# Attention and state space steps moved between the quarters of the projection

## What is computed

```python
h = x @ w_in
z, xbc, dt_raw, q, k, v = _split(h, [1024, 1536, 16, 512, 512, 512])
xbc = jax.nn.silu(_causal_depthwise_conv(xbc, conv_w, conv_b))        # 4 taps
dt = jax.nn.softplus(dt_raw + dt_bias); a = -jnp.exp(a_log)
y = _ssd_scan(xs, dt, a, bs, cs)                                      # 16 heads of 64, 2 groups
y = _rms_norm((y + d_skip * xs) * jax.nn.silu(z), norm_g)
# stick-breaking attention, 8 heads of 64, strictly causal:
#   A[t,s] = sigmoid(z_ts) * prod_{s<j<t} (1 - sigmoid(z_tj))
return jnp.concatenate([y, sb], axis=-1) @ w_out
```

## Time and profile before

| | us |
|---|---|
| median of 3 runs | 2407.09 (2406.55 to 2411.23) |
| the profiled execution, its own time | 2406.45 |
| its span in the trace | 2404.6 |
| PE busy in the span | 2195.6 |
| DVE busy | 1760.2 |
| ACT busy | 1399.7 |
| mean granted clock of TensorE | 0.945 |

### The profile page before, as it was taken

How to read it: one execution, slowest core, us unless ns; L and a number is a source line. 1 busy time by engine, 2 the same in 40 slices (tenths; PEclk the granted TensorE clock), 3 DMA queues, 4 the chain that set the end, 5 groups by cost and what they waited for, 6 DMA issues and landing times.

```text
span 2404.6 us, 31268 instructions
## 1 busy us (share of the span) xinstructions
PE 2195.6 (91%) x9954; PEld 1753.4 (73%) x9954; DVE 1760.2 (73%) x2376; ACT 1399.7 (58%) x1832; POOL 77.2 (3%) x76
## 2 busy tenths in 40 slices
PE   8858899799899797899987799999999999999998
PEld 7846577676677584588776478787878787878886
DVE  5554498764789643445566479898989898989897
ACT  4434277444477340244454168787878787878785
POOL 1000100000100000011110100000000000000000
PEclk9866899999799898999999789999999999999999
DMA  6400588342487242564232089898989898989895
GB/s 237 176 1 0 221 322 335 129 168 108 159 340 280 88 163 92 220 243 174 88 137 74 0 342 376 329 370 326 376 327 377 322 374 323 381 320 380 317 387 220
DMA packets 81542, 577.09 MB, mean 240 GB/s; under 512 B 9408, under 2 KB 9408, under 8 KB 12992
## 3 DMA queue, kind: packets, MB, share of 16 engines
q1 hardware_dynamic: 79888, 570.40, 60.9%
q0 software_dynamic: 1584, 5.77, 0.7%
HBM read 575.08 MB, written 1.05 MB: 240 GB/s over the span
## 4 chain that ended last, share of the span: by engine, by line
PE 77%; DVE 13%; issue 5%; ACT 3%; DMA 1%; POOL 1%; DVEq 0%; SPq 0%; ACTq 0%; POOLq 0%
PE bank L467 21%; PE bank L469 20%; PE bank L468 20%; PE bank L585 6%; PE bank L1221 1%; DVE h L1579 1%; DVE dn_lo L1527 1%; PE bank L1187 1%; DVE pj_lo L504 1%; DVE gu_lo L1527 1%; PE bank L1260 1%; PE bank L572 1%; ACT dn_hi L1364 1%; ACT gu_hi L1356 1%; DMA pieces<-in_pieces 1%
## 5 line engine op out<-in xcount | busy, mean ns | idle before, releaser
L1527 DVE TENSOR_TENSOR gu_lo<-ffw_gu,gu_hi 128x1024 fp32r<-128x1024 f32 x620 | 755.0, 1237 | 145.1 <-ACT gu_hi L1356 130.7
L1356 ACT CAST gu_hi<-ffw_gu 128x1024 fp32r<-128x1024 f32 x620 | 648.1, 1052 | 195.8 <-DMA ffw_gu<-in_gate_up_ff 70.6
L467 PE MATMUL bank<-gu_hi,xg_lo 128*128 128x512 f32 x1152 | 463.0, 402 | 4.5 <-DVE xg_lo L1527 4.3
L469 PE MATMUL bank<-gu_hi,xg_hi 128*128 128x512 f32 x1152 | 452.5, 393 | 0.0
L468 PE MATMUL bank<-gu_lo,xg_hi 128*128 128x512 f32 x1152 | 451.7, 392 | 0.0
L1527 DVE TENSOR_TENSOR dn_lo<-ffw_d,dn_hi 128x1024 fp32r<-128x1024 f32 x299 | 362.7, 1221 | 58.3 <-ACT dn_hi L1364 48.8
L1364 ACT CAST dn_hi<-ffw_d 128x1024 fp32r<-128x1024 f32 x310 | 325.3, 1055 | 95.3 <-PE bank L469 91.6
L467 PE MATMUL bank<-dn_hi,hidt_lo 128*128 128x512 f32 x664 | 265.5, 400 | 28.8 <-DVE hidt_lo L1527 28.8
L469 PE MATMUL bank<-dn_hi,hidt_hi 128*128 128x512 f32 x664 | 259.8, 391 | 0.0
L468 PE MATMUL bank<-dn_lo,hidt_hi 128*128 128x512 f32 x664 | 259.6, 391 | 0.0
L467 PEld LDWEIGHTS bank<-gu_hi,xg_lo 128*128 128x128 f32 x1152 | 217.9, 189 | 48.0 <-DVE xg_lo L1527 5.3
(11 more groups left out here) (394 smaller groups left out, 2852.7 us busy)
## 6 DMA issues: line engine op xcount, KB each, us to landing
ffw_gu<-in_gate_up_m SPq DMA_DIRECT2D x288, 1024.0 KB, 7.0
ffw_d<-in_down_m SPq DMA_DIRECT2D x144, 1024.0 KB, 7.7
pieces<-in_pieces SPq DMA_DIRECT2D x70, 1024.0 KB, 7.1
ffw_gu<-in_gate_up_ff SPq DMA_DIRECT2D x22, 1024.0 KB, 7.0
ffw_d<-in_down_ff SPq DMA_DIRECT2D x11, 1024.0 KB, 8.9
pieces<-in_pieces SPq DMA_DIRECT2D x4, 512.0 KB, 7.3
norm_vec<-in_ln_g POOLq DMA_DIRECT2D x4, 512.0 KB, 4.0
norm_vec<-in_ln_b POOLq DMA_DIRECT2D x4, 512.0 KB, 5.4
```

The source lines that it names most:

```text
L467: nc.tensor.matmul(bank, a_lo, b_hi, start=start, stop=False)
L469: return nc.tensor.matmul(bank, a_hi, b_hi, start=False, stop=stop)
L1356: nc.scalar.copy(gu_hi[:, 2 * k:2 * k + 2, :], ffw_gu[:, blk["slot"], 2 * k:2 * k + 2, :])\
L1527: return V.tensor_tensor(out, x, hi.bitcast(F32), ALU.subtract)
```

## The change

The pieces come in the order q, k, v, dt, xbc (columns 1024 to 1535, which are B and C, first), z, z. A quarter is numbered `at` = 4n + k for piece n and quarter k, 0 to 35. `project_quarter` is the old loop body, and between quarters the engines do:

- the stick-breaking attention in eleven slots (`SB_AT`), from quarter 9 to quarter 21. A head is no longer computed by logarithms. ACT takes two sigmoids of the logits (of z and of -z), DVE forms the product of the (1 - sigmoid)s backward with two `tensor_tensor_scan`s over reversed rows, with a `diagonal` of ones that restarts it, and multiplies; PE turns the weights (three transposes) and ACT copies them out;
- softplus of dt at 16 to 22, with one table that holds exp and ln;
- the convolutions at 20 to 31; their first tap is on ACT (`conv_tap_scalar`), and so are all evacuations of the banks;
- the products of B and C at 25, the first third of `ev_mixT` at 26;
- the state space part for group 0 at 28 to 32 and for group 1 at 33 to 37, five steps (`ssd_tensor`, `ssd_scalar`, `ssd_vector`). The products of `above` and `da` are on ACT (`steps_scalar`, 32 instructions of 128x128) and no more on DVE;
- 36 and 37 lie between the matmuls of the first third of the output, which needs attention alone. The gates, the squares for the rms norm (on ACT) and its roots come there too.

After these, 16 transposes and the other two thirds of the output follow. In the odd mixer a preload of the table with exp and ln is added ahead of its log of the forget gate. Three masks of the attention are gone. The core of the diff:

```diff
@@ -85,14 +85,13 @@
...
-    even = [("z", "tok", columns("ev_w_in", 0, 512), 512), ("z", "tok", columns("ev_w_in", 512, 1024), 512)]
-    even += [("xbc", "feat", columns("ev_w_in", o + 512 * i, o + 512 * (i + 1)), 512) for i in range(3)]
-    o += CONV_DIM
-    even += [("dt", "tok", columns("ev_w_in", o, o + SSD_H), SSD_H)]
-    o += SSD_H
-    even += [("q", "feat", columns("ev_w_in", o, o + 512), 512), ("k", "feat", columns("ev_w_in", o + 512, o + 1024), 512),
-             ("v", "tok", columns("ev_w_in", o + 1024, o + 1536), 512)]
-    even_out = [rows("ev_w_out", k) for k in range(3)]
+    q0 = o + CONV_DIM + SSD_H
+    even = [("q", "feat", columns("ev_w_in", q0, q0 + 512), 512), ("k", "feat", columns("ev_w_in", q0 + 512, q0 + 1024), 512),
+            ("v", "tok", columns("ev_w_in", q0 + 1024, q0 + 1536), 512),
+            ("dt", "tok", columns("ev_w_in", o + CONV_DIM, o + CONV_DIM + SSD_H), SSD_H)]
+    even += [("xbc", "feat", columns("ev_w_in", o + 512 * i, o + 512 * (i + 1)), 512) for i in (2, 0, 1)]
+    even += [("z", "tok", columns("ev_w_in", 0, 512), 512), ("z", "tok", columns("ev_w_in", 512, 1024), 512)]
+    even_out = [rows("ev_w_out", k) for k in (2, 0, 1)]
...
     def project_piece(pe, t, n, first_bank):
 
-            _, kind, g, cols = PLANS[t][n]
-            for k in range(4):
-                if n == 0:
-                    pe.wait_ge(sem("x_split"), DC // 2 * MIXER[t] + k + 1)
...
+        for k in range(4):
+            project_quarter(pe, t, n, k, first_bank)
+
+    def project_quarter(pe, t, n, k, first_bank):
+
+        _, kind, g, cols = PLANS[t][n]
+        if n == 0:
+            pe.wait_ge(sem("x_split"), DC // 2 * MIXER[t] + k + 1)
...
+    EV_N = len(even_pieces)
+    SB_AT = {4 * n + k: i for i, (n, k) in enumerate(((2, 1), (2, 2), (2, 3), (3, 1), (3, 3), (4, 0), (4, 1), (4, 2), (4, 3),
+                                                      (5, 0), (5, 1)))}
+    CONV_AT = 20
+    CONV_ORDER = (8, 9, 10, 11, 0, 1, 2, 3, 4, 5, 6, 7)
+    SSD_AT = (28, 33)
+
+    def ssd_step(at):
+
+        return [(g, at - SSD_AT[g]) for g in range(SSD_G) if 0 <= at - SSD_AT[g] < 5]
+
+    def ssd_tile(g, s):
+
+        return s // 2, 2 * g + s % 2
...
+    def sb_slot_tensor(pe, i):
+        if i < SB_H:
+            if i == 0:
+                pe.wait_ge(sem("const_ready"), 1)
+                read_wait(pe, "ev", 0, 2)
+                read_wait(pe, "ev", 1, 2)
+            if i >= 2:
+                pe.wait_ge(sem("sb_taken"), i - 1)
+            q, kk, bank = (sbq_odd if i % 2 else sbq_even)[:, i // 2, :], sbk[:, i // 2, :], psum[4 + i % 2]
+            nc.tensor.matmul(bank[:, 0:P], q[:, 0:P], kk[:, 0:P], start=True, stop=True)
+            nc.tensor.matmul(bank[:, P:3 * P], q[:, P:S], kk, start=True, stop=True).then_inc(sem("sb_logits"), 1)
+        if 2 <= i < SB_H + 2:
...
+            if v >= 1:
+                pe.wait_ge(sem("sb_wt"), v)
+            for b in range(3):
+                last = nc.tensor.transpose(psum[6][:, b * P:(b + 1) * P], sb_w[:, v % 2, b, :], ident)
+            last.then_inc(sem("sb_turned"), 1)
+        if i >= 3:
+            v = i - 3
+            pe.wait_ge(sem("sb_wt"), v + 1)
...
+                pe.wait_ge(sem("sb_out_read"), 1)
+            for b, (j, s) in enumerate(TRI):
+                at = (v % 4) * P + j * HD
+                last = nc.tensor.matmul(psum[7][:, at:at + HD], sb_wT[:, v % 2, b, :], sbv[:, s, v * HD:(v + 1) * HD],
+                                        start=(s == 0), stop=(s == j))
+            last.then_inc(sem("sb_out"), 1)
...
+    def sb_slot_scalar(act, i):
+        if i == 7:
+            sb_out_scalar(act, 0)
+        if i < SB_H:
+            act.wait_ge(sem("sb_logits"), i + 1)
+            if i >= 2:
+                act.wait_ge(sem("sb_weighted"), i - 1)
+            z = psum[4 + i % 2][:, 0:3 * P].rearrange("p (b t) -> p b t", b=3)
+            nc.scalar.activation(sb_take[:, i % 2], z, ACT.Sigmoid)
+            nc.scalar.activation(sb_pass[:, i % 2], z, ACT.Sigmoid, scale=-1.0).then_inc(sem("sb_taken"), 1)
...
+        if 2 <= i < SB_H + 2:
+            v = i - 2
+            act.wait_ge(sem("sb_turned"), v + 1)
+            if v >= 2:
+                act.wait_ge(sem("sb_out"), v - 1)
+            nc.scalar.copy(sb_wT[:, v % 2], psum[6][:, 0:3 * P].rearrange("p (b t) -> p b t", b=3)).then_inc(sem("sb_wt"), 1)
+        if i == SB_H + 2:
+            sb_out_scalar(act, 1)
+
+    def sb_slot_vector(dve, i):
+        v = i - 1
+        if not 0 <= v < SB_H:
+            return
+        dve.wait_ge(sem("sb_taken"), v + 1)
+        if v >= 2:
+            dve.wait_ge(sem("sb_turned"), v - 1)
+        take, left, w_ = sb_take[:, v % 2], sb_pass[:, v % 2], sb_w[:, v % 2]
+        flat, one = left.rearrange("p b t -> p (b t)"), diagonal.rearrange("p b t -> p (b t)")
+        late, early = flat[:, 3 * P - 1:P - 1:-1], flat[:, P - 1::-1]
+        vlink(V.tensor_tensor_scan(out=late, data0=late, data1=one[:, 2 * P - 1::-1], initial=0.0, op0=ALU.mult, op1=ALU.add))
+        vlink(V.tensor_tensor_scan(out=early, data0=early, data1=one[:, 2 * P - 1:P - 1:-1], initial=0.0, op0=ALU.mult,
+                                   op1=ALU.add))
+        vlink(V.tensor_tensor(w_[:, :, 0:P - 1], take[:, :, 0:P - 1], left[:, :, 1:P], ALU.mult))
+        vlink(V.tensor_tensor(w_[:, 1, P - 1:P], take[:, 1, P - 1:P], left[:, 2, 0:1], ALU.mult), sem("sb_weighted"))
...
+    def ssd_tensor(pe, g, r):
+        base = 4 * g
+
+        def seg(s, bank):
+            pe.wait_ge(sem("ev_steps"), base + s + 1)
+            for i in range(4):
+                last = nc.tensor.matmul(psum[bank][:, i * P:(i + 1) * P], steps[:, s % 2, i, :], upto, start=True, stop=True)
+            last.then_inc(sem("ev_seg"), 1)
+
+        def diag(s):
+            j, q = ssd_tile(g, s)
+            pe.wait_ge(sem("ev_weights"), base + s + 1)
+            pe.wait_ge(sem("ev_tok_read"), 2 * g + j + 1)
+            for i in range(4):
+                at, head = (s % 2) * 256 + i * SSD_P, 4 * q + i
+                last = nc.tensor.matmul(psum[4 + j][:, at:at + SSD_P], decay[:, s, i, :],
+                                        xdt[:, j, head * SSD_P:(head + 1) * SSD_P], start=True, stop=True)
+            last.then_inc(sem("ev_diag"), 1)
+        if r == 0:
+            pe.wait_ge(sem("ev_conv_out"), 8 + 4 * g)
+            for j in range(T):
+                if g:
+                    pe.wait_ge(sem("ev_y_read"), j + 1)
+                elif j == 0:
+                    pe.wait_ge(sem("ev_cbm"), 1)
+                else:
+                    pe.wait_ge(sem("ev_btok"), 1)
+                for i in range(4):
+                    last = nc.tensor.transpose(psum[4 + j][:, i * P:(i + 1) * P], xc[:, 4 * g + i, TILES[j]], ident)
+                last.then_inc(sem("ev_tok_turned"), 1)
+            if g == 0:
+                pe.wait_ge(sem("mixt_read"), 2)
+            else:
+                pe.wait_ge(sem("ev_off_read"), 1)
+            seg(0, 6)
+            seg(1, 7)
+        if r == 1:
+            pe.wait_ge(sem("ev_decay"), base + 1)
...
+        if r == 2:
+            diag(0)
+            diag(1)
+            pe.wait_ge(sem("ev_state"), g + 1)
+            seg(3, 6)
+        if r == 3:
+            pe.wait_ge(sem("ev_decay"), base + 3)
+            nc.tensor.matmul(psum[7], xc[:, 10 + g, P:S], state[:, g * 512:(g + 1) * 512], start=True, stop=True)\
+                .then_inc(sem("ev_off"), 1)
+            diag(2)
+        if r == 4:
+            diag(3)
...
+        for c in range(4):
+            last = nc.tensor.matmul(psum[2 * j + half], ev_mixT[:, k, c, TILES[j]],
+                                    piece_ap(even_out[k])[:, c, half * 512:(half + 1) * 512],
+                                    start=(k == 0 and c == 0), stop=(k == 2 and c == 3))
+        return last
 
     def even_tensor(pe):
...
+        for n in range(EV_N):
             if n >= 2:
-                pe.wait_ge(sem("ev_tok_read"), n - 1)
...
+                read_wait(pe, "ev", 0, n - 1)
+                read_wait(pe, "ev", 1, n - 1)
+            for k in range(4):
+                project_quarter(pe, "ev", n, k, 2 * (n % 2))
+                at = 4 * n + k
+                if at in SB_AT:
+                    sb_slot_tensor(pe, SB_AT[at])
+                if at == 21:
+                    pe.wait_ge(sem("sb_taken"), SB_H)
+                    pe.wait_ge(sem("ev_dt"), 2)
+                    dav = da.rearrange("p j h -> p (j h)")
+                    nc.tensor.matmul(psum[4][:, 0:32], upto, dav, start=True, stop=True)
+                    nc.tensor.matmul(psum[4][:, 32:64], above, dav, start=True, stop=True).then_inc(sem("ev_cum"), 1)
+                if at == 25:
+                    pe.wait_ge(sem("ev_conv_out"), 4)
+                    for i in range(4):
+                        j, g = divmod(i, SSD_G)
```

(112 more changed lines are left out.)

493 lines of the change are left out of this document (199 added, 294 removed).

## The result

The changed kernel takes 2330.64 us (median of 4 runs, 2328.35 to 2332.38) where the kernel before takes 2407.05: 0.9679 of it, 95% interval 0.9667 to 0.9691. That is 76.4 us less. The forecast was 66.7 less, and its range ended at 2331, 0.4 us above the median. The profiled executions have spans of 2404.6 and 2328.7. The gain depends on the chip by some us, since the kernel before does: on the three chips of the experiments its medians are 2411.5, 2414.15 and 2408.41 us, and on the first of them 17 executions lie in two groups, eight from 2404 to 2407 and nine from 2411.5 to 2415. The changed kernel was 77.4 us faster on the third (experiment 12), and the variants of experiments 2 and 8, whose edits show no effect, were 82.7 and 85.0 faster on the first two.

What follows compares the result with a forecast made beforehand. PE bound the kernel, waiting or at a low clock between projection and output, with one head in flight. −115.6 + 39.5 + 3 + 3 − 3.0 + 6.4 = −66.7 us gave 2340 us; range 2331 to 2362.

Steps and rivals of the forecast that it cites:

- four stages removed: Between last projection and first output matmul: state space steps, gates, attention, norm and transposes leave the path, −115.6 us.
- PE's work moved between quarters: Attention, dt sums, B and C work, transposes and state space steps added to PE within the projection: +39.5 us.
- stalls and handovers: Quarters 28 to 31: 3 us of PE waits for silu and weighting, plus 3 us for handovers between engines.
- clock in the dt piece: fp32 matmul slots in and behind this piece hold the clock: −2.1 us behind it, −0.9 for dt, together −3.0.
- tail: After the last quarter: remaining steps within the output's first third, 16 transposes, then the rest of the output; +6.4 us.
- What follows moves forward as a block: Everything behind the even mixer's output keeps its times and only starts earlier; nothing is taken for the odd mixer's preload.
- its own sign: The prediction is wrong if the clock falls below 0.9 between quarters 12 and 35.
- rival 1: Gates' quarters: ACT and DVE bound them, eight quarters at 2 us more, 2356 us; chance 0.20.
- rival 2: Quarters 28 to 31: silu and exp table switches cost ACT 2.6 us each, 8 over PE, 2348 us; chance 0.05.
- rival 3: Quarters 28 to 35: the clock drops and 38 us of PE work double, 2378 us; chance 0.05.
- rival 4: Attention: reversed scans on DVE cost so much that the kernel is slower, above 11.3 us a head; chance 0.03.
- rival 5: A wait in one engine's order makes quarters serial again, or the following stage does not move: 2404 us; chance 0.01.

Runs made afterwards that it cites:

- experiment 12: The changed kernel run again, unedited, and the source of its second profile: 2331.05 us.
- experiment 2: The changed kernel without the added line that preloads ACT's exp and ln table in the odd mixer: 2328.76 us.
- experiment 8: The changed kernel with ACT's exp table preloaded at the end of the even mixer, for the routing of the experts: 2329.12 us.
- experiment 1: The changed kernel with the three transposes of each head's attention weights issued four times over, 72 transposes more: 2335.16 us.
- experiment 3: The kernel before with only the odd mixer's table preload line added: 0.9994 of the time without it.
- experiment 11: The kernel before with the 24 transposes ahead of its first output matmuls issued four times over, delaying what follows: 1.0039 of the kernel before.
- experiment 5: The changed kernel with the attention's eleven slots in one block behind quarter 15, not between quarters: 2336.74 us.
- experiment 10: The changed kernel with attention slots at quarters 9 to 11 and 16 to 23, none in the dt piece: 2331.35 us.
- experiment 4: The changed kernel with ACT's eight products for group 0 moved from quarter 27 to quarter 24: 2323.71 us.
- experiment 7: The changed kernel with the last four convolutions' silus together in quarter 32, four table loads fewer in quarters 28 to 31: 2328.68 us.

## Why the prediction was wrong, point by point

The direction, the mechanism and most terms were right; the time was 9 us too high, from two steps. In the table the second row is not a reading: it is the prediction's own sum with a transpose at 0.12 instead of 0.24. The clock row is what the prediction took for the kernel before's loss, 3.0, less the loss in the window shown (11 x 0.14 is 1.5 to 1.6; in experiment 12, whose quarter 25 is 2.9 us later, 4.5).

| term, us | predicted | from the first profile |
|---|---|---|
| four stages removed | −115.6 | −115.6 |
| PE's work moved between quarters | +39.5 | +33.3, with transposes at 0.12 |
| stalls and handovers | +6 | +6.0 (5.2 in quarters 28 to 32, 0.8 for L811) |
| clock in the dt piece | −3.0 | −1.4 (+1.5 in the second profile) |
| tail | +6.4 | +5.2 |
| to the end of the mixer | −66.7 | −72.0 (−69.0 in the second) |
| behind it | 0 | −3.9 |

The measured terms before the tail sum to 37.9, where 38.4 passed (111.38 to 149.77); 0.5 is not placed.

**The first step that failed is the price of a transpose.** The prediction took "three transposes 0.72" and "eight transposes of attention for the output: 1.9", the 0.24 us of an fp32 matmul of 128 columns. Experiment 1 shows 0.11 in a row, and the first of a batch adds a little: eight take 0.97 (L915) to 1.09 (L877). 68 transposes, 52 in the projection and 16 in the tail, were 0.12 too dear each: 8.2 us. With that alone the sum is −74.9, 2332. The trace of before could have told it. 48 matmuls of L585 are x96, but the 24 transposes of L572 leave 24 records:

```profile
221.50 5.49 PE bank L572 x24
```

This is 0.23 us each at a clock of 0.52 (from 215 us), so an estimated 0.12 at full clock.

**The second is "What follows moves forward as a block".** Nothing behind was edited that shows: no gain of the preload can be seen (experiments 2 and 3), and the routing's extra load is hidden (8). Yet the stages there took other times, because the clock fell at other places in them. The odd mixer took 138.3 and 138.5 us in the two profiles with the timing of the kernel before, and 132.4 to 136.2 in the twelve others, which start it at other times; one of them is experiment 11, with the code of before. From the norm's first vector to the end the kernel before takes 2128.3, the changed one 2124.4 and 2124.3, eight of its nine variants 2119.8 to 2125.1 and the ninth (5) 2128.7. The kernel before with the preload takes 2126.2, experiment 11 2126.9. So the 3.9 us between the two first profiles are within what this unedited part varies by, and no merit of the change's own work. Which moment makes the clock fall I can't tell from these runs.

**The clock in the dt piece** was reasoned wrongly. The slots of fp32 matmuls don't hold it (10). It fell in every profile, for 4 us in two, longer in the others; predicted −3.0, measured −1.4 and +1.5. This partly hid the error of the transposes. The −0.9 within it was also small by its own numbers: 3.3 us at 0.61 lose 1.3. By its own sign (a clock below 0.9 between quarters 12 and 35) the prediction failed here too: 0.86 over the dt piece, and 0.63 from 112 to 116 us.

**Stalls:** the named one, the silu behind evacuation and eight products, was predicted at 2 and is 2.16 us; experiment 4 takes away all but 0.33 of it. The eight products ahead of the silu took 2.45 us where the prediction had 2.0. The 3 us of unnamed handovers are there as well, but not as handovers: 1.5 of them are the clock that falls behind this very wait. That the sum came out at 6.0 is in part luck. The one on the weighting (predicted 1 us) is 0.4.

**Table switches:** six loads of 1.28 in quarters 28 to 31, the next activation 0.01 to 0.02 us behind five of them (in the chain above 117.71 + 1.28 = 118.99, and the silu starts at 119.00) and 0.08 behind the first. By this the drain of 1.38 us that the Trainium skill gives (ScalarE: Activation LUTs, section What ACT_TABLE_LOAD costs) does not show here. Four of them, 5.1 us of ACT, cost PE 1.5 to 1.6 us (7).

**Scans:** 0.69 + 0.42 us a head, the 1.1 that was taken. The rule of the Trainium skill that the built-in scan runs at half throughput (DVE: opcode table, instruction layouts, handler registers and perf-mode slots, section Datapath and trigger behaviour) agrees with it roughly: 256 elements take 0.69 us, 2.7 ns each, and an ordinary multiplication of 381 takes 0.56, 1.5 ns each.

**Rivals:** 1 did not come as eight quarters at 2 us more: quarters 33 to 35 take 15.6 us, PE's own work. In quarters 28 to 32 ACT does lead, at the 5.2 us that the forecast nearly had. 2 falls by its rows. 3 came on a small scale, 1.5 us. (Its 38 us of PE work are 40.7 by the prediction's own terms, 20.8 + 19.9. And the serial steps ran at full-clock prices only towards their end: the stage stood at 0.76.) 4 and 5 are out. The norm hides in the first third with 1.5 us to spare (scaling ends at 164.6, the third at 166.15), as forecast.

## What to carry over

Price a transpose by its own row: count the records of one batch against the number of instructions in the code before a price of one kind is used for another. Work put between quarters of another stage gains most where that work was a serial chain; of the attention's gain here, more came from the cheaper chain with two heads in flight and its better clock (24 us) than from its place (6 to 9). Once PE has no long wait left, look at what stands ahead of its next releaser in that engine's order: moving eight instructions by three quarters gave 3.1 us.

## What the runs showed of the hardware

The granted clock falls for some microseconds in the same code at one start and not at another: in the odd mixer this is worth up to 6 us (132.4 to 138.5), and in the dt piece 3 (97.28 and 100.19 us for the same kernel). Single profiles of two kernels that differ in timing can't be compared stage by stage below that. Nor are their ends alike: from the last norm vector (asked for at 920 us in experiment 4, 1003 in experiment 11) to the end, unedited code took 1401.2 to 1402.3 us in eleven profiles and 1403.5, 1407.1 and 1410.0 in the other three. A short wait can cost more than its length: 2.2 us of waiting were followed by eight matmuls at 3.25 us instead of 1.8. It was so in seven profiles of eight; in experiment 1 the same wait left the clock up. Twelve fp32 transposes of 128x128 take 1.31 us, four fp32 matmuls of that size 0.95.
